# First modulation units of 512 shift and 512 scale columns, three projection blocks by quarters of K, x loaded first, unit 4 on TensorE

## The chip, the core and the metric

The kernel runs on one core of a Trainium2 chip. Its engines are TensorE (matrix products), VectorE, ScalarE, GpSimd and SyncE (SP), which here only starts DMAs; the core's 16 DMA engines move the data. The metric is the device time of one execution in microseconds, as the median of several runs.

## The reference

Two blocks of a network on 256 tokens of 2048 features, in float32. The change is in the first stages of the first block:

```python
mod = silu(c) @ w_ada + b_ada            # 12288 columns: six parts of 2048
shift_mix, scale_mix, gate_mix, shift_ffn, scale_ffn, gate_ffn = split(mod, 6)
h = modulate(rmsnorm(x, g_norm_mix), shift_mix, scale_mix)   # h * (1 + scale) + shift
u = h @ w_in                             # 2048 x 3072: lru, pool and gate columns, 1024 each
lru: causal conv of width 4, two gates by heads of 64, recurrence, times gelu(gate columns)
pool: four sliding means minus the input, times w_pool
x = x + gate_mix * (concat(lru, pool) @ w_out)
x = x + gate_ffn * ffn(modulate(rmsnorm(x), shift_ffn, scale_ffn))
```

The second block (state space and attention mixer, its own feed-forward, and a gated embedding) follows and is not touched.

## The kernel before

**Modulation.** The 12288 columns of `w_ada` are taken in twelve units of 1024 columns (`MOD_COLS`); a unit is 16 tiles of 128 rows of K, 512 KB each. Units 0 and 1 are the shift of the first norm, 2 and 3 its scale. `MOD_ORDER` (line 157) takes the first four as 0, 2, 1, 3, so that after two of them shift and scale of features 0 to 1023 are there, and after four the rest. For these TensorE multiplies: `mod_product` (line 1702) is two matmuls of 32 columns of weights by 512 (four instructions in the trace, since float32 takes two passes) for each tile, and two neighbouring tiles use different columns of the array. ScalarE then copies the sums to `mod_rows` (`mod_out`, line 1021 on), TensorE turns them to features by partitions (`mod_turn`, line 1690), VectorE adds the bias (`first_result`). The tiles come by SP's queue into eight slots (`load_first`, line 623), each asked for when the product eight before is done. `x` is loaded behind tile 4 and tile 5.

The other eight units are paced: `mod_places` says how many of their tiles stand at each place of `w_in` and `w_out`. GpSimd starts their loads into six slots (line 600), the first when all 64 first products are done. Units 5 and 6 are multiplied by TensorE in pairs of tiles (`mod_pair`, line 1719), the others, unit 4 among them, by VectorE into `mod_acc` (line 2464), and summed over partitions by TensorE (`mod_sums`, line 1663).

**Norm and `w_in`.** `x` is squared and scaled by ScalarE into `xn`, turned by TensorE (`turn_block`) into `features`. Two chunks of features at a time (`q`), VectorE applies gain and shift (`scaled`), ScalarE rounds to the high part `a_hi` (`norm_high`), VectorE takes the rest `a_lo` (`norm_low`). `w_in` is 6 blocks of 512 columns; each block is 8 halves, a half being 2 chunks of K. A 1 MB tile of `w_in` holds two halves and comes by SP's queue into one of four slots of `raw` (`load_tile`). Each half is split by ScalarE (`split_hi`, L845) and VectorE (`split_lo`, L2242) into high and low parts, three halves ahead of TensorE, and multiplied with 24 matmuls (`features_half`, lines 1538 to 1540: high by high, low by high, high by low). So each multiplies 8 times a line for a half, and the whole of `w_in` is 48 halves.

Halves are counted by places. Places 0 to 15 are blocks 0 and 1 done together: halves 0 to 3 of block 0, then of block 1 (the first half of K, which the first two units allow), then halves 4 to 7 of both. Six of the first four stand beside the first products at `W_IN_AT`, two after them. From place 8 on, `mods_beside` puts the pairs of paced tiles between the halves, one place behind (`MOD_LAG`). Block 0 and 1 are the lru columns: their conv taps are read from PSUM by VectorE (L2405) and must be done before block 2 or 3 writes the same bank of `pair`. The gates' products (line 1814) stand behind block 2, those of the pool (line 1790) in block 5. Then `w_out`, four blocks of eight halves (lines 1556 to 1558), its last instructions being `mod_joint` (line 1676).

All engines run in the order written here and wait for each other by semaphores.

Of the kernel before, what the change touches and what calls it, by code (L numbers as in the profile page):

```python
# [26 lines left out]
P = 128  # L27
# [60 lines left out]
def two_blocks(nc, d, out):  # L88
# [55 lines left out]
    def ya_slot(k):  # L144
# [69 lines left out]
    with ExitStack() as ctx:  # L214
# [38 lines left out]
        xn_sq = at("xn_sq", F + 32, [P, T, D])  # L253
# [14 lines left out]
        mod_more = [at("mod_more_0", 88, [P, 2, MOD_COLS]), at("mod_more_1", 104, [P, 2, MOD_COLS])]  # L268
# [237 lines left out]
        MOD_TURN_AT = [(1, 8), (2, 3), (3, 3)]  # L506
        TURN0_AT, W_IN_AT = [(1, 9), (1, 13), (2, 1), (2, 4)], [(2, 12), (2, 15), (3, 2), (3, 5), (3, 8), (3, 11)]
# [42 lines left out]
        def _(pool):  # L550
# [71 lines left out]
        def _(sp):  # L622
            def load_first(s):
                if s >= FIRST_SLOTS:
                    sp.wait_ge(mod_used, s - FIRST_SLOTS + 1)
                sp.dma_start(first_slot(s), ada[:, s % KC, bass.ds(MOD_ORDER[s // KC] * MOD_COLS, MOD_COLS)]).then_inc(mod_landed[s % FIRST_SLOTS], 16)
# [38 lines left out]
            sp.dma_start(c_rows[0:KC, :], by_chunk(d["c"][0])).then_inc(c_landed, 16)  # L665
            def load_in(b, j):
# [4 lines left out]
            w_in_at = {2 * KC + 3: 0, 2 * KC + 9: 1, 2 * KC + 15: 2, 3 * KC + 5: 3}  # L671
            for s in range(MOD_FIRST * KC):
# [159 lines left out]
        def _(act):  # L832
# [69 lines left out]
            def norm_sums(n, b):  # L902
# [3 lines left out]
                else:  # L906
                    mod_out(MOD_SUMS.index(7) + 1, JOINT_USED, misc[:, 3, :])
# [120 lines left out]
            def first_out(i):  # L1028
                mod_out(i, KC * (i + 1), first_bank(i))
# [5 lines left out]

            act.wait_ge(vec_turned, 1)
# [2191 lines left out]
```

## Time and profile before

| | us |
|---|---|
| median of 3 runs | 2527.49 (2527.4 to 2527.76) |
| span of the profiled execution | 2526.6 |
| TensorE busy in it | 2496.0 |
| VectorE busy | 1631.2 |
| ScalarE busy | 1257.4 |

The profile gives for each engine its busy time and, for each idle time, which engine or transfer ended it. The granted clock is TensorE's, as a share of 2.4 GHz. The DMA share is the mean busy share of the 16 DMA engines; queue q1 is the one that SP's loads use, q0 the one of GpSimd's. A matmul's row has its start and its modelled length; as matmuls overlap, the distance from start to start is what one costs.

### The profile page before, as it was taken

The numbers are of one execution on the slowest core, as the hardware profiler recorded it, in microseconds if no ns is written. First come the engines' busy times: TensorE is split into PE (matmuls) and PEld (weight loads), VectorE is DVE, ScalarE is ACT, GpSimd is POOL, SyncE is SP. The second block draws the span as 40 slices with busy tenths as digits, with TensorE's granted clock in tenths as the row PEclk, the third lists the DMA queues.
The fourth block names the chain that finished last, engine by engine and source line by source line (L and its number), as shares of the span: only waits on it lengthen the run. The fifth ranks groups of instructions, "written<-read, shape, count | busy, mean of one in ns | idle before, by whom it ended". The sixth has DMA issues, their size and how long they took to land.

```text
span 2526.6 us, 31728 instructions
## 1 busy us (share of the span) xinstructions
PE 2496.0 (99%) x12066; PEld 2032.2 (80%) x12066; DVE 1631.2 (65%) x1989; ACT 1257.4 (50%) x1665; POOL 78.7 (3%) x165
## 2 busy tenths in 40 slices
PE   7999999999999999999999999999999999999999
PEld 1688878888888888888888888888888888888887
DVE  1468998765555555565788678556777777755545
ACT  2354455444444444454566656445555555544463
POOL 0012210100000000000000000000000000000000
PEclk9999999999999999999999999999999999999999
DMA  9999998976666666675544554766777777766664
GB/s 383 394 345 384 358 353 295 327 262 221 213 219 220 201 215 211 211 217 176 167 132 132 179 192 167 229 206 229 237 247 238 240 237 241 237 210 203 212 233 133
DMA packets 401644, 600.34 MB, mean 238 GB/s; under 512 B 20944, under 2 KB 244208, under 8 KB 401024
## 3 DMA queue, kind: packets, MB, share of 16 engines
q1 hardware_dynamic: 381024, 525.66, 62.9%
q0 software_dynamic: 19616, 71.34, 7.5%
q10 hardware_dynamic: 896, 1.84, 0.3%
q8 instruction: 74, 1.21, 0.2%
q14 instruction: 34, 0.28, 0.0%
HBM read 573.84 MB, written 24.94 MB: 237 GB/s over the span
## 4 chain that ended last, share of the span: by engine, by line
PE 93%; DMA 3%; DVE 2%; ACT 1%; issue 1%; SPq 0%; POOL 0%; DVEq 0%; ACTq 0%
PE pair L1556 28%; PE pair L1558 27%; PE pair L1557 27%; DMA mod_raw<-in_w_ada 2%; PE pair L1538 1%; PE misc L1706 1%; PE pair L1539 1%; PE pair L1540 1%; DVE w_lo L2242 1%; PE misc L2102 1%; PE misc L1940 1%; DMA mod_page<-in_w_ada 0%; PE misc L1931 0%; PE misc L1919 0%; DMA mod_more<-in_w_ada 0%
## 5 line engine op out<-in xcount | busy, mean ns | idle before, releaser
L2242 DVE TENSOR_TENSOR w_lo<-raw,w_hi 128x1024 fp32r<-128x1024 f32 x848 | 1015.1, 1203 | 739.3 <-ACT w_hi L845 736.7
L845 ACT ACTIVATE w_hi<-raw 128x1024 fp32r<-128x1024 f32 x848 | 882.5, 1043 | 954.6 <-PE pair L1558 869.3
L1556 PE MATMUL pair<-w_hi,a_hi 128*128 128x512 f32 x2016 | 791.3, 393 | 0.8 <-DVE w_lo L2242 0.7
L1558 PE MATMUL pair<-w_hi,a_lo 128*128 128x512 f32 x2016 | 785.1, 389 | 0.0
L1557 PE MATMUL pair<-w_lo,a_hi 128*128 128x512 f32 x2016 | 784.5, 389 | 0.0
L1556 PEld LDWEIGHTS pair<-w_hi,a_hi 128*128 128x128 f32 x2016 | 378.4, 188 | 82.8 <-issue 2.9
L1558 PEld LDWEIGHTS pair<-w_hi,a_lo 128*128 128x128 f32 x2016 | 378.4, 188 | 79.2
L1557 PEld LDWEIGHTS pair<-w_lo,a_hi 128*128 128x128 f32 x2016 | 378.6, 188 | 77.4 <-issue 0.5
L1556 PE MATMUL pair<-w_hi,hid_hi 128*128 128x512 f32 x704 | 274.0, 389 | 0.0
L1558 PE MATMUL pair<-w_hi,hid_lo 128*128 128x512 f32 x704 | 273.9, 389 | 0.0
L1557 PE MATMUL pair<-w_lo,hid_hi 128*128 128x512 f32 x704 | 273.9, 389 | 0.0
L1557 PEld LDWEIGHTS pair<-w_lo,hid_hi 128*128 128x128 f32 x704 | 132.1, 188 | 27.6
L1556 PEld LDWEIGHTS pair<-w_hi,hid_hi 128*128 128x128 f32 x704 | 132.1, 188 | 27.6
L1558 PEld LDWEIGHTS pair<-w_hi,hid_lo 128*128 128x128 f32 x704 | 132.1, 188 | 27.3
L1538 PE MATMUL pair<-a_hi,w_hi 128*128 128x256 f32 x384 | 111.6, 291 | 1.4 <-DVE xc L2405 1.1
L1539 PE MATMUL pair<-a_lo,w_hi 128*128 128x256 f32 x384 | 108.5, 283 | 0.0
L1540 PE MATMUL pair<-a_hi,w_lo 128*128 128x256 f32 x384 | 108.5, 283 | 0.0
L1538 PEld LDWEIGHTS pair<-a_hi,w_hi 128*128 128x128 f32 x384 | 73.4, 191 | 18.2 <-issue 13.5
L2464 DVE SCALAR_TENSOR_TENSOR mod_acc<-mod_raw,keep,mod_acc 128x1024 f32<-128x1024 f32 x60 | 76.7, 1278 | 11.1 <-DMA mod_raw<-in_w_ada 10.3
L1539 PEld LDWEIGHTS pair<-a_lo,w_hi 128*128 128x128 f32 x384 | 73.6, 192 | 0.1
L1540 PEld LDWEIGHTS pair<-a_hi,w_lo 128*128 128x128 f32 x384 | 73.5, 191 | 0.0
L600 POOL DMA_DIRECT2D mod_raw<-in_w_ada x86 | 45.6, 531 | 337.4 <-DVE mod_acc L2464 146.3
(400 smaller groups left out, 2165.6 us busy)
## 6 DMA issues: line engine op xcount, KB each, us to landing
raw<-in_w_in SPq DMA_DIRECT2D x88, 1024.0 KB, 5.4
raw<-in_w_up SPq DMA_DIRECT2D x176, 512.0 KB, 4.4
raw<-in_w_out SPq DMA_DIRECT2D x48, 1024.0 KB, 5.7
raw<-in_w_ffn_gate SPq DMA_DIRECT2D x88, 512.0 KB, 3.6
raw<-in_w_ffn_up SPq DMA_DIRECT2D x88, 512.0 KB, 4.6
mod_raw<-in_w_ada POOLq DMA_DIRECT2D x86, 512.0 KB, 7.5
raw<-in_w_ffn_down SPq DMA_DIRECT2D x32, 1024.0 KB, 5.1
raw<-in_w_down SPq DMA_DIRECT2D x32, 1024.0 KB, 5.1
```

The costliest lines, as they stand in the source:

```text
L600: pool.dma_start(mod_slot(n), ada[:, k, bass.ds(a * MOD_COLS, MOD_COLS)]).then_inc(page_landed[mod_landing(n)[0]], 16)
L845: run(w_hi[:, h % HALF_SLOTS, 0:n, :], raw[:, h // 2 % RAW_SLOTS, at0:at0 + n, :], ACT.Copy).then_inc(hi_ready, 1)
L1538: pe.matmul(o, wh, hi[:, k, :], start=(kh == kk == 0 and m % 2 == 0), stop=False, skip_group_check=True)
L1539: pe.matmul(o, wh, lo[:, k, :], start=False, stop=False, skip_group_check=True)
L1540: mm = pe.matmul(o, wl, hi[:, k, :], start=False, stop=(kh == ph.halves - 1 and kk == n - 1), skip_group_check=True)
L1556: pe.matmul(o, hi[:, own], w_hi[:, slot, kk, :], start=(h == kk == 0), stop=False)
L1557: pe.matmul(o, hi[:, own], w_lo[:, slot, kk, :], start=False, stop=False)
L1558: mm = pe.matmul(o, lo[:, own], w_hi[:, slot, kk, :], start=False, stop=(h == ph.halves - 1 and kk == n - 1))
L1706: mm = pe.matmul(bank[own], c_silu[:, k:k + 1].to_broadcast([P, P // 4]), tile[:, e * COLS:(e + 1) * COLS], start=(k < 2), stop=(k >= KC - ...
L1940: mm = pe.matmul(misc[HD * e:HD * (e + 1), 2 + q, 3 * P:], v_t[:, k, n, :], p_tr[:, i % 2, e, keys], start=(k == 0), stop=(k == q), skip_g ...
L2242: dve.tensor_tensor(w_lo[:, slot, 0:n, :], raw[:, h // 2 % RAW_SLOTS, at0:at0 + n, :], w_hi[:, slot, 0:n, :].bitcast(F32), ALU.subtract).t ...
L2464: dve.scalar_tensor_tensor(out=acc, in0=of, scalar=by, in1=acc, op0=ALU.mult, op1=ALU.add).then_inc(mod_step, 1)
```

## The change

- **Units.** Each of the first four units `u` now holds 512 shift columns and the 512 scale columns of the same features (`by_quarter`). A tile is still 512 KB, in two pieces of 512 columns for each row of K. After unit `u` the features of quarter `u` can be finished: `first_result`, gain and `scaled` work by quarters.
- **`w_in`.** Blocks 0, 1 and 2 are done together by quarters of K: six halves for each quarter (`in_half`). Halves 6(u-1) to 6(u-1)+4 stand beside the products of unit `u` (`W_IN_AT`), the sixth behind its `mod_turn`; the last six follow unit 3. Block 2 is accumulated in `misc[:, 0:2]`, blocks 0 and 1 in `pair`. SP puts three tiles of `w_in` in each unit's loads.
- **`x` first.** `x` is loaded ahead of the first tile, and `xn` is computed by VectorE. The vectors are turned after product 6 and the features at products 7, 9, 11 and 13 of unit 0.
- **Paced units.** Unit 4 goes to TensorE. `mods_by_place` states the tiles of each place (D for VectorE, P for TensorE), from place 18 on. GpSimd's first six loads wait for 57 to 62 products instead of 64. The eight first slots lie elsewhere (`mod_more` in one piece).
- **Around it.** Conv, gates (behind place 26), pool and gelu steps keep their order and stand at new places.

```diff
-    mod_places = [0] * 8 + [0, 3, 1, 3, 0, 2, 0, 3] + [1, 2, 1, 2, 1, 0, 1, 1] + [1, 3, 2, 1, 1, 1, 2, 1] + [3, 2, 2, 2, 0, 2, 1, 2] \
-        + [2, 1, 3, 2, 1, 1, 2, 1] + [2, 1, 1, 2] + [1, 1, 1, 2] * 6 + [0] * 4 + [1, 0] * (4 * up1.halves)
-    MOD_ORDER = [0, 2, 1, 3]
-    MOD_BY_PE, MOD_BY_DVE = [5, 6], [4, 7, 8, 9, 10, 11]
+    FIRST_BLOCKS = 3
+    FIRST_HALVES = 2 * FIRST_BLOCKS
+    FIRST_PLACES = FIRST_BLOCKS * w_in.halves
+    PACED = FIRST_PLACES - FIRST_HALVES - 1
+
+    mods_by_place = [""] * (PACED + 1) + ["DPP", "DPP"] + ["PP"] * 6 + ["D", "DD", "D", "PP", "DPP", "D"] \
+        + ["PP", "D", "PP", "PP", "PP", "PP", "PP", "D"] + ["PP", "D", "PP", "D", "D", "PP", "PP", "D"] \
+        + ["DPP", "D", "DPP", "DD", "DPP", "D", "DPP", "DD"] + ["D", "D", "D", "DD"] * 4 + ["D"] * 4 + [""] * 4
+    mod_places = [len(m) for m in mods_by_place]
+    MOD_BY_PE, MOD_BY_DVE = [5, 4, 6], [7, 8, 9, 10, 11]
...
     def in_half(p):
 
-        b, h = divmod(p, w_in.halves)
-        return (b, h) if b >= 2 else (h // 4, 4 * b + h % 4)
+        q, n = divmod(p, FIRST_HALVES)
+        return divmod(p, w_in.halves) if p >= FIRST_PLACES else (n // 2, 2 * q + n % 2)
...
+        def in_bank(block):
+
+            return misc[:, 0:2] if block == FIRST_BLOCKS - 1 else pair[:, 1 - block % 2] if block < FIRST_BLOCKS else pair[:, block % 2]
...
-        MOD_TURN_AT = [(1, 8), (2, 3), (3, 3)]
-        TURN0_AT, W_IN_AT = [(1, 9), (1, 13), (2, 1), (2, 4)], [(2, 12), (2, 15), (3, 2), (3, 5), (3, 8), (3, 11)]
+        TURN0_AT, W_IN_AT = [7, 9, 11, 13], {3: (0, 1), 7: (2,), 11: (3,), 15: (4,)}
+        GATES_AT = 26
...
                 if n < MOD_SLOTS_LATER:
-                    pool.wait_ge(mod_used, FIRST_TILES)
+
+                    pool.wait_ge(mod_used, FIRST_TILES - FIRST_SLOTS + n + 1)
...
-                sp.dma_start(first_slot(s), ada[:, s % KC, bass.ds(MOD_ORDER[s // KC] * MOD_COLS, MOD_COLS)]).then_inc(mod_landed[s % FIRST_SLOTS], 16)
+                u, k = divmod(s, KC)
+                sp.dma_start(first_slot(s).rearrange("p (e n) -> p e n", e=2),
+                             by_quarter(ada[:, k, 0:2 * D], u)).then_inc(mod_landed[s % FIRST_SLOTS], 16)
...
-            w_in_at = {2 * KC + 3: 0, 2 * KC + 9: 1, 2 * KC + 15: 2, 3 * KC + 5: 3}
+            w_in_at = {u * KC + s: FIRST_BLOCKS * u + n for u in range(MOD_FIRST) for n, s in enumerate((12, 15, 19))}
...
             pe.wait_ge(c_ready, 1)
-            for i in range(MOD_FIRST):
+            for u in range(MOD_FIRST):
+                p = FIRST_HALVES * (u - 1)
                 for k in range(KC):
-                    first_product(i, k)
...
+                    first_product(u, k)
+                    if u == 0:
+                        if k == 6:
+                            turn_vectors()
+                        elif k in TURN0_AT:
+                            turn_block(0, TURN0_AT.index(k))
+                    else:
+                        for n in W_IN_AT.get(k, ()):
+                            if (u, n) == (1, 4):
+
+                                pe.wait_ge(n_f, XB)
+                            half_in(p + n)
+                mod_turn(u, u + 1)
+                if u:
+                    half_in(p + FIRST_HALVES - 1)
...
+            for u in range(MOD_FIRST):
+                p = FIRST_HALVES * u
+                split_in(range(max(0, p - 2), p + 2))
+                first_result(u)
+                dve.wait_ge(mod_ready, u + 1)
+                modulated_gain(mod[:, KC:2 * KC], g_mix, slice(4 * u, 4 * u + 4))
+                for q in (2 * u, 2 * u + 1):
+                    scaled(q)
+                for q in (2 * u, 2 * u + 1):
+                    norm_low(q)
+                if u < MOD_FIRST - 1:
+                    split_in(range(p + 2, p + 4))
+                if u == 0:
+                    prepare_lru()
+                    prepare_cosines()
```

## Rows read from the trace of the kernel before

**Rows 1.** The page: busy time of engines, and the span in 40 slices

```profile
PE   7999999999999999999999999999999999999999
...
DMA  9999998976666666675544554766777777766664
```

**Rows 2.** TensorE's waits, before 76 us, then 149.8 to 364: us, times, longest

```profile
PE pair L1706 <- DMA mod_more<-in_w_ada: 7.4, 11, 2.7
PE pair L1706 <- DMA mod_raw<-in_w_ada: 4.6, 7, 2.2
...
PE pair L1556 <- DVE w_lo L2242: 0.9, 2, 0.5
```

**Rows 3.** Stretches: length; busy PE, PEld, DVE, ACT, POOL; clock, DMA share, GB/s

```profile
2.00:8.00 6.00, 3.13 (x11) 0.77 (x13) 0.00 (x0) 0.28 (x2) 2.40 (x17) 1.00 0.94 342
...
60.00:80.00 20.00, 15.36 (x78) 6.28 (x80) 7.50 (x14) 5.15 (x7) 0.00 (x0) 0.83 1.03 402
...
96.00:104.00 8.00, 8.00 (x60) 5.72 (x57) 1.23 (x1) 0.02 (x1) 0.00 (x0) 1.00 1.03 404
104.00:108.00 4.00, 3.26 (x29) 1.62 (x28) 0.00 (x0) 0.60 (x1) 1.05 (x2) 1.00 1.05 388
...
300.00:320.00 20.00, 20.00 (x96) 16.66 (x95) 19.89 (x19) 9.99 (x13) 4.23 (x8) 1.00 1.04 399
...
149.80:363.90 214.10, 212.66 (x1358) 182.77 (x1356) 180.40 (x173) 106.10 (x135) 40.66 (x77) 1.00 0.97 363
0.00:149.80 149.80, 127.06 (x787) 70.50 (x788) 52.75 (x106) 49.88 (x61) 15.65 (x46) 0.94 1.01 382
```

**Rows 4.** TensorE from 149.8 to 364 us, groups by line: count, busy us, mean ns

```profile
L1538 PE MATMUL pair<-a_hi,w_hi 128*128 128x256 f32 x240 | 69.6, 290 | 0.0
L1706 PE MATMUL misc<-mod_raw,keep 128*32 128x512 f32 x68 | 10.6, 603 | 0.0
L1706 PE MATMUL misc<-mod_page,keep 128*32 128x512 f32 x28 | 5.3, 603 | 0.5 <-DMA mod_page<-in_w_ada 0.5
L1667 PE MATMUL misc<-ones,mod_acc 128*128 128x1 f32 x32 | 3.8, 248 | 0.0
```

**Rows 5.** TensorE in order of time: start us, us, what, count, idle before

```profile
107.32 1.05 PE L1698 MATMUL misc<-keep,mod_rows 128*128 128x2 f32 x8 [0.74 <-ACT mod_rows L1026]
...
123.35 1.06 PE L1706 MATMUL misc<-mod_raw,keep 128*32 128x512 f32 x8
124.35 0.39 PE L1538 MATMUL pair<-a_hi,w_hi 128*128 128x256 f32 x1
...
149.82 0.28 PE L1538 MATMUL pair<-a_hi,w_hi 128*128 128x256 f32 x1
...
363.94 1.06 PE L1676 MATMUL misc<-mod_acc,ones 128*32 128x512 f32 x8
```

**Rows 6.** DMA queues in 110 to 111, then 111 to 112 us: packets, MB, share

```profile
q1 hardware_dynamic: 200, 0.39, 105.8%
...
q0 software_dynamic: 61, 0.25, 63.4%
q1 hardware_dynamic: 66, 0.13, 35.0%
```

**Rows 7.** GpSimd in order of time

```profile
106.95 2.24 POOL L600 DMA_DIRECT2D mod_raw<-in_w_ada  x4 [75.30 <-PE misc L1706]
```

**Rows 8.** VectorE and ScalarE in order of time behind the last turn

```profile
108.82 1.45 DVE L2500 TENSOR_SCALAR features<-features,keep,mod 128x256 f32<-128x256 f32 x4
110.33 0.69 DVE L2338 TENSOR_TENSOR a_lo<-features,a_hi 128x512 fp32r<-128x512 f32 x1
...
109.66 1.28 ACT L932 ACTIVATE a_hi<-features 128x512 fp32r<-128x512 f32 x2 [2.39 <-DVE features L2500]
```

**Rows 9.** DMA of 120 to 160 us: mean, and GpSimd's issues with landing in us

```profile
DMA packets 7342, 14.25 MB, mean 356 GB/s; under 512 B 2425, under 2 KB 2425, under 8 KB 7338
...
mod_raw<-in_w_ada POOLq DMA_DIRECT2D x12, 512.0 KB, 9.9
```

More of the change, by code:

```diff
@@ L665, in _ @@
             sp.dma_start(c_rows[0:KC, :], by_chunk(d["c"][0])).then_inc(c_landed, 16)
+            for t in range(T):
+                sp.dma_start(x[:, t, :], d["x"][0, t * P:(t + 1) * P, :]).then_inc(x_landed, 16)
             def load_in(b, j):
@@ L689, in load_gates @@
                              w.rearrange("(m e) i j -> e i m j", e=2)[e]).then_inc(mixw_landed, 16)
-            for b in range(1, w_in.blocks):
-                if b == 2:
+            for b in range(FIRST_BLOCKS, w_in.blocks):
+                if b == FIRST_BLOCKS:
                     sp.wait_ge(zeroed, 2)
@@ L1046, in _, with split_in, prepared @@
[L1046 to L1048 removed]
+            def split_in(places):
+                for p in places:
+                    ph, b, h = in_or_out(p)
+                    split_hi(ph, b, [h])
+            def prepared():
+                act.wait_ge(prep_in, 1)
+                run(l_exp, l_abs, ACT.Exp, scale=-1.0).then_inc(prep_exp, 1)
+                act.wait_ge(prep_in, 2)
+                run(half_sin, ang_r, ACT.Sin, scale=0.5).then_inc(prep_exp, 1)
+                run(sin_t, ang_r, ACT.Sin).then_inc(prep_exp, 1)
@@ L1065, in mixer @@
-            def mixer(b):
-                for n in range(w_in.halves):
-                    h = LEAD + n
-                    ph, b1 = (w_in, b) if h < w_in.halves else (w_in, b + 1) if b + 1 < w_in.blocks else (w_out, 0)
-                    split_hi(ph, b1, [h % w_in.halves])
-                    if (b, n) == (1, 4):
-                        act.wait_ge(w_used, w_in.half(1) + 4)
-                        conv_bias(0, 0, cw1[:, (CONV - 1) * RC:], cb1, xc, c1_bias)
-                    beside(b, n)
-                    rows_beside(b * w_in.halves + n)
-                act.wait_ge(w_used, w_in.end(b))
@@ new lines, in beside @@
+            def beside(p):
+                if p == 20:
+                    act.wait_ge(w_used, 20)
+                    conv_bias(1, 0, cw1[:, (CONV - 1) * RC:], cb1, xc, c1_bias)
+                elif p == 22:
+                    act.wait_ge(w_used, 22)
+                    conv_bias(0, 4, cw1[:, (CONV - 1) * RC:], cb1, xc, c1_bias)
+                elif p == 24:
+                    act.wait_ge(w_used, 24)
+                    run(flat(xp[:, 0:4, :]), flat(misc[:, 0:2, :]), ACT.Copy).then_inc(xp_ev, 1)
+                elif p == 26:
+                    run(std, var, ACT.Sigmoid)
+                elif p == 27:
+                    for m in range(RC):
+                        act.wait_ge(gate_mm, m + 1)
+                        run(lru_a[:, m, :], misc[:, m % 3, 0:S], ACT.Sigmoid, bias=b_ra[:, m:m + 1]).then_inc(gate_ev, 1)
+                        run(lru_u[:, m, :], misc[:, m % 3, S:2 * S], ACT.Sigmoid, bias=b_ri[:, m:m + 1]).then_inc(gate_ev, 1)
+                elif p == 29:
@@ L2624, in pooled_out @@
                                              op0=ALU.mult, op1=ALU.subtract).then_inc(pool_lo_ev, 1)
-            for b in range(1, w_in.blocks):
-                mixer(b)
+            for p in range(PACED, IN_PLACES):
+                split_in([p + LEAD])
+                beside(p)
+                mod_beside(p)
             pooled_out(range(6, 2 * G))
```

248 lines of the change are left out of this document (99 added, 149 removed).

## The prediction

> **What bounds the kernel now.** I read the page first, then TensorE's waits by stretch, then the stretches with their granted clock and DMA rate, then TensorE's own order of time. The page says that TensorE is busy for 99% of the span and that only the first of the 40 slices is open, and that the DMA engines are full in the first seven slices, up to about 440 us [rows 1]. The reader is to see that the change touches only the first 364 us: the last 32 tiles of the paced units and all that comes after `w_out` keep their count and order. TensorE waits for `w_ada` tiles by DMA 12.0 us before 76 us in the two largest groups alone (7.4 + 4.6), and between 149.8 and 364 us it waits 1.4 us in all (0.9 for VectorE, 0.5 for a tile) [rows 2, 4]. So up to the first half of `w_in` at about 76 us DMA sets the pace and TensorE has room, and after it TensorE does: 214.1 us with 212.7 busy [rows 3, 4].
>
> The time is therefore a sum of two parts: when TensorE gets to a fixed place of its work, and how much it still has to do from there. I take as that place the start of half 18 of the 48 halves of `w_in` (the place from which the new code goes on by blocks, and the last quarter of K begins). Before, it starts at 149.82 us; 240 of the 384 matmuls of line 1538 are left (30 halves of 8), and 96 of line 1706, 4 instructions to a tile, so 24 tiles or 12 pairs [rows 4, 5]. From there to the end of `w_out`, the matmuls of line 1676 at 363.94, it is 214.1 us.
>
> **The change, part by part.**
>
> Bytes before the last first-unit tile. The 64 tiles of 512 KB are 33.55 MB, `x` 2.10 MB. SP now puts ten 1 MB tiles of `w_in` (10.49 MB) ahead of tile 63, against four before. Sum 46.1 MB. They all run on queue q1.
>
> Rate. A tile of `w_ada` is now two pieces of 512 columns in each row, so its runs in HBM are 2 KB and no longer 4 KB; those of `w_in` are 2 KB already. At 96 to 104 us, with nearly only 4 KB runs moving, the row gives 404 GB/s; at 104 to 108, with only `w_in` tiles in flight, 388, at a full share in both [rows 3]. I take 388 for the 44.0 MB and 404 for `x`, whose runs are longer: 113.4 + 5.2 us. The start costs 3.7 us, an estimate: 2 us and some before the first transfer, and of the 2 to 8 us at 342 GB/s [rows 3] one us is lost. So without any rival traffic tile 63 lands at 3.7 + 5.2 + 113.4 = 122.3 us. The ends are 404 GB/s for all (117.8 us) and 388 with the same start loss as now (123.7).
>
> The Trainium skill (DMA: Bandwidth & Descriptors, "Why small descriptors are slow") tells of a fixed cost of some 3 cycles a packet beside one cycle for each 32 bytes. By that 2 KB would cost 67 cycles twice where 4 KB costs 131, or 2.3%, and 44 MB would take 110.2 us at the rate of the 4 KB row less 2.3%, 3 us less than by the row. The trace shows 4%, and the sum goes by the trace.
>
> GpSimd's tiles. POOL now asks for the first six tiles of the paced units when 57, 58 ... products are done, not after 64. Before, its first request was issued at 106.95 us and its queue q0 moved nothing until 111; in the microsecond 110 to 111 q1 had 200 packets, in the next q0 had 61 and q1 66 [rows 6, 7]. So the data follow some 4.5 us behind the request, and then the two queues take turns packet by packet, with 4 KB on q0 against 2 KB on q1: q0 gets 0.25 MB of each us and q1 0.13. In the new order product 56 comes after half 14, at about 115.5 us (tile 55 lands at 3.7 + 5.2 + 38.8 MB / 388 GB/s = 108.9, but TensorE is at halves 12 and 13 until 110, does products 52 to 55 in 2 us, half 14 until 115). Pool data then flow from 120. Of q1 0.8 MB are still to come, and at 0.13 MB/us that takes 6 us in place of 2: tile 63 lands at 126. The ends: 122 if the requests come late enough to miss it, 130 if all six tiles (3.1 MB, 8 us at 390) go ahead of it.
>
> TensorE in the same stretch. A half is 24 matmuls at 0.12 us, 2.88 us; a pair of products 0.99 us start to start (123.35 to 124.35) [rows 4, 5]. A unit has 16 products (8 us in pairs, some more when they come one by one), a turn of 1.0 and six halves of 17.3: 27 us. DMA needs for a unit 8.39 + 3.15 MB at 388, 29.7 us. So 18 halves (52 us of work) lie beside transfers where 6 did; TensorE has some 2.5 us of room in each unit. ScalarE and VectorE have 6 splits of 1.04 and 1.2 us in a unit of 30 us each, and the normalisation of `x` that moves from ScalarE to VectorE is early and hidden by the arrival of unit 0. The turn of the vectors moves from after product 13 to after product 6 and may wait for small loads until some 22 us; eight tiles are in flight by then, so no transfer is late.
>
> From tile 63 to half 18: product 0.98, half 16 2.88 (it covers ScalarE's copy of the rows), turn 1.05, half 17 2.88; in all 7.8. Beside half 17 runs the chain bias, gain, four scalings 1.45, high part 0.63, low part 0.69, which before took from the turn's end at 108.37 to 111.0 [rows 5, 8]: 2.7 us, hidden with 0.2 to spare. What comes next if it is late is the same wait, tenths of a us. Half 18 then starts at 126 + 7.8 = 133.8, against 149.8: 16.0 us earlier.
>
> Unit 4 on TensorE. Sixteen tiles are eight more pairs, and unit 6's all lie behind half 18 too, as do all of unit 5's: 24 pairs after it against 12 before. 12 x 0.99 = 11.9 us, and all of it on the path, since TensorE is full there. For unit 4 the sums over `mod_acc` (line 1667: 3.8 us for two units) give way to a turn of 1.0: 0.8 less or so [rows 4, 5]. VectorE is freed of 16 x 1.28 us, worth nothing unless it is the bound; in `w_out`, where it is busy 19.9 of 20 us [rows 3], it has 34 tiles against 36, and TensorE waits for it 0.9 us [rows 2]. The four gates' loads (small runs), the conv taps, gates and pool steps move by some places; each stands again three or more halves ahead of its reader. I cost them at nothing; 0.5 us each if not.
>
> Waits behind half 18. The eight pairs of places 18 to 25 are read every 3.87 us from six slots, so a slot has 11.6 us from read to next read; landing takes a median of 9.9 us in the stretch 120 to 160 [rows 9], and issue another 0.5 to 1. Most are in time by a us; the first pair after the six that are in hand is asked for at 141 and read at 147, 1 to 2 us late. I put 3 us for all such waits, where before has 1.4. Bounds 0 and 8.
>
> **Sum.** -16.0 + 11.9 - 0.8 + 1.6 = -3.3 us on the profiled span of 2526.6, 2523.3; the median of the three runs, 2527.5, lies 0.9 above that span, so 2524.2.
>
> **The rivals.**
>
> B, DMA is quicker than I take it: 2 KB runs at 404 GB/s (-4.4 us), q0 doesn't overtake (-4), or one of these with fewer waits behind half 18. Against it speak [rows 3, 6]; for it, that in `w_out`, with both kinds of runs mixed, 399 is reached. One and a half of these: -3.3 - 6.5, 2517.7.
>
> C, slower: DMA becomes the bound of the whole stretch to the end of `w_out`. Before, 57.2 MB were in by 149.8 us and 77.7 came after (382 and 363 GB/s [rows 3]). Of the same 134.9 MB now 50.7 are in at 133.8, and 84.2 are left for 226.6 us, a mean of 372 GB/s, where 363 at a share of 0.97 was moved before and 399 in the best part. The work decides for TensorE down to 366 GB/s at the cost of the gain; at 356, the mean of 120 to 160 us with the gates' loads [rows 9], 84.2 MB take 236.5 us, end 370.3, so +6.4: 2533.9. For it: q1 and q0 are both full in `w_out` already. Against: the last 4.2 MB are tiles of `up1` that need not be in by then, and the ten slots hold 7.3 MB in hand.
> The Trainium skill (same page, "Where 436 GB/s comes from") says that the HBM side binds at some 358 GB/s for each core. By that C would hold, with 84.2 MB in 235 us and 2532.4. The rows of 404 and 399 GB/s here speak against it, so it adds nothing to C's chance.
>
> D, slower: the halves aren't hidden by the transfers. If TensorE has a clock of 0.83 (between its two levels of 1.2 and 2.4 GHz), as in the stretch 60 to 80 us [rows 3], the 82 us of work in the three units take 17 us more, of which 7.5 are room: +9.5, 2533.7. Before 76 us single waits are as long as 2.7 and 2.2 us; from 96 us on, where they are short, the clock is 1.00 [rows 2, 3]. The new order fills such gaps, so this is unlikely. Also here: that the change doesn't do what it says, and a quarter's first halves wait for the chain of mod rows, so that fewer than 18 are done when tile 63 lands; each half that is left costs 2.9.
>
> **How the numbers follow.** Forecast 0.46 (2520 to 2528), B 0.27, C 0.16, D 0.11. A measurement of this kernel tells some 0.2%, 5 us, from no change. Faster by more than that: a third of the forecast's chance and nearly all of B, 0.41. Slower: two thirds of C, most of D, 0.20. Same: 0.39. The range leaves a tenth on either side: 2514 to 2534.
>
> **What would show it.** In the profile after: the first matmul of line 1538's kind at 39 to 43 us; DMA at 385 to 395 GB/s from 12 to 110 us; tile 63's products at 124 to 130; half 18 at 132 to 138; 24 pairs in place of 12 behind it with about 11 us more of line 1706's work; the end of `w_out` at 358 to 363; 2163 us from there as before. Wrong if the DMA rate of the first 110 us is over 400 or under 375, if q0 moves nothing before tile 63, if TensorE waits more than 8 us behind half 18, or if anything after `w_out` changes length.

## The result, and the profile after

| | before | after |
|---|---|---|
| median, same chip | 2527.73 us (2527.36 to 2529.11) | 2535.35 us (2533.46 to 2537.32) |
| profiled execution: time, span | time not kept, 2526.6 | 2535.05, 2533.3 |
| half 18 of `w_in` starts | 149.82 | 141.41 |
| `w_out` ends | 363.94 | 370.59 |

The ratio is 1.0029, with a 95% interval of 1.002 to 1.0038: slower, by 7.6 us. The prediction was 3.3 us faster; its range ended at 2534. The traces of the two kernels differ by less, 6.7 us. Wherever both are kept, the time is 1.7 to 2.0 us above the span, so the execution behind the trace of before took some 2528.3 us (an estimate), 0.6 above its median here. Lines moved: the products are L1724, the matmuls of a half L1556 to L1558, the turn L1716, GpSimd's loads L616.

First the place the prediction named, half 18. TensorE of the changed kernel in order of time, from the first half of `w_in` to the last quarter of K (start, length, what, count, idle before and what ended it):

```profile
39.44 5.79 PE L1724 MATMUL misc<-mod_raw,keep 128*32 128x512 f32 x16 [0.95 <-DMA mod_raw<-in_w_ada]
45.16 0.39 PE L1556 MATMUL pair<-a_hi,w_hi 128*128 128x256 f32 x1
...
123.41 1.05 PE L1724 MATMUL misc<-mod_more,keep 128*32 128x512 f32 x4 [1.27 <-DMA mod_more<-in_w_ada]
127.13 1.92 PE L1724 MATMUL misc<-mod_more,keep 128*32 128x512 f32 x4 [2.66 <-DMA mod_more<-in_w_ada]
130.96 1.92 PE L1724 MATMUL misc<-mod_more,keep 128*32 128x512 f32 x4 [1.91 <-DMA mod_more<-in_w_ada]
132.81 0.58 PE L1556 MATMUL misc<-a_hi,w_hi 128*128 128x256 f32 x1
...
136.18 0.41 PE L1556 MATMUL misc<-a_hi,w_hi 128*128 128x256 f32 x1
136.39 0.41 PE L1557 MATMUL misc<-a_lo,w_hi 128*128 128x256 f32 x1
...
141.41 0.28 PE L1556 MATMUL pair<-a_hi,w_hi 128*128 128x256 f32 x1
...
147.26 1.06 PE L1724 MATMUL misc<-mod_raw,keep 128*32 128x512 f32 x8
151.32 1.06 PE L1724 MATMUL misc<-mod_page,keep 128*32 128x512 f32 x8
```

The first half of `w_in` starts at 45.16 us, where the prediction had 39 to 43: the first four products of unit 1 take 5.8 us, mostly at the low clock. That was made up for, since TensorE waits for tiles again at 63 us. The last two rows are pairs of paced tiles, with one half behind each. The last three tiles of the 64 come 2.3 to 3.8 us apart. Behind the wait of 2.66 us a product takes 1.92 us in place of 1.05, and in half 16 two matmuls stand 0.21 us apart in place of 0.12: half 16, from 132.81 to the turn at 137.64, lasts 4.8 us and not 2.9. The stretches show the clock (columns as in [rows 3]):

```profile
20.00:40.00 20.00, 13.61 (x84) 6.08 (x82) 6.62 (x18) 7.16 (x9) 1.81 (x1) 0.95 1.05 385
40.00:60.00 20.00, 20.00 (x136) 12.27 (x133) 10.01 (x29) 8.07 (x11) 0.00 (x0) 0.88 1.05 387
...
126.00:130.00 4.00, 1.92 (x4) 0.18 (x4) 0.00 (x0) 0.00 (x0) 0.00 (x0) 0.60 1.03 399
130.00:134.00 4.00, 3.04 (x9) 1.38 (x10) 0.00 (x0) 0.60 (x1) 0.00 (x0) 0.50 1.03 399
134.00:138.00 4.00, 4.00 (x25) 4.00 (x24) 0.00 (x0) 0.00 (x0) 0.00 (x0) 0.62 1.05 386
...
141.30:370.60 229.30, 225.78 (x1449) 184.15 (x1447) 175.46 (x179) 111.30 (x145) 47.68 (x90) 1.00 0.96 358
```

From 130 to 134 us the granted clock is 0.50, the lower of its two levels, 1.2 GHz. In the first rows, with 2 KB runs, DMA gives 385 to 387 GB/s where before has 402 to 404 [rows 3]. GpSimd's requests, and what the queues did in 122 to 124 us:

```profile
117.30 2.25 POOL L616 DMA_DIRECT2D mod_raw<-in_w_ada  x4 [93.46 <-PE misc L1724]
122.45 0.53 POOL L616 DMA_DIRECT2D mod_page<-in_w_ada  x1 [2.91 <-PE misc L1724]
...
q0 software_dynamic: 143, 0.52, 66.3%
q1 hardware_dynamic: 139, 0.28, 36.3%
```

143 packets of the one and 139 of the other queue: they take turns, and GpSimd's are nearly twice as large (3.6 and 2.0 KB on average). While its tiles come, the first 64 get 36% of the engines' time.

Behind half 18, the waits of TensorE in 141 to 371 us:

```profile
PE misc L1724 <- DMA mod_raw<-in_w_ada: 2.8, 2, 1.9
PE misc L1724 <- DMA mod_page<-in_w_ada: 0.8, 1, 0.8
```

So half 18 came 8.4 us earlier than before, not 16.0, and the way from there to the end of `w_out` is 229.2 us where it was 214.1; TensorE is busy for 225.7 of them. From there to the end both kernels take 2162.7 us.

### The profile page after: what moved, and what is told of

Same layout as the page of the kernel before. It is cut to its first block, busy times and chain, and to the rows that moved or that the text cites. A ratio compares the mean times of both kernels' runs of the same rounds, so it can differ in the third digit from the quotient of the medians.

```text
span 2533.3 us, 31826 instructions
## 1 busy us (share of the span) xinstructions
PE 2496.7 (99%) x12122; PEld 2033.6 (80%) x12122; DVE 1619.1 (64%) x1977; ACT 1254.8 (50%) x1664; POOL 78.8 (3%) x165
## 4 chain that ended last, share of the span: by engine, by line
PE 94%; DMA 3%; DVE 1%; SPq 1%; ACT 0%; issue 0%; POOL 0%; DVEq 0%
PE pair L1574 27%; PE pair L1576 27%; PE pair L1575 27%; PE misc L1724 2%; DMA mod_more<-in_w_ada 2%; PE pair L1556 1%; DMA mod_raw<-in_w_ada 1%; PE pair L1557 1%; PE pair L1558 1%; PE misc L2117 1%; PE misc L1955 1%; PE misc L1946 0%; PE misc L1934 0%; PE misc L1556 0%; PE misc L1557 0%
## 5 line engine op out<-in xcount | busy, mean ns | idle before, releaser
L1556 PE MATMUL pair<-a_hi,w_hi 128*128 128x256 f32 x320 | 93.4, 292 | 0.0
L1557 PE MATMUL pair<-a_lo,w_hi 128*128 128x256 f32 x320 | 90.4, 283 | 0.0
L1558 PE MATMUL pair<-a_hi,w_lo 128*128 128x256 f32 x320 | 90.4, 282 | 0.0
L1556 PEld LDWEIGHTS pair<-a_hi,w_hi 128*128 128x128 f32 x320 | 61.1, 191 | 18.3 <-issue 16.6
L2479 DVE SCALAR_TENSOR_TENSOR mod_acc<-mod_raw,keep,mod_acc 128x1024 f32<-128x1024 f32 x53 | 67.8, 1279 | 10.5 <-DMA mod_raw<-in_w_ada 10.2
L1557 PEld LDWEIGHTS pair<-a_lo,w_hi 128*128 128x128 f32 x320 | 61.3, 192 | 0.1
L1558 PEld LDWEIGHTS pair<-a_hi,w_lo 128*128 128x128 f32 x320 | 61.2, 191 | 0.0
L616 POOL DMA_DIRECT2D mod_raw<-in_w_ada x86 | 45.7, 533 | 348.0 <-PE misc L1724 156.7
```

The lines of the kernel that those rows point to most:

```text
L616: pool.dma_start(mod_slot(n), ada[:, k, bass.ds(a * MOD_COLS, MOD_COLS)]).then_inc(page_landed[mod_landing(n)[0]], 16)
L1556: pe.matmul(o, wh, hi[:, k, :], start=(kh == kk == 0 and m % 2 == 0), stop=False, skip_group_check=True)
L1557: pe.matmul(o, wh, lo[:, k, :], start=False, stop=False, skip_group_check=True)
L1558: mm = pe.matmul(o, wl, hi[:, k, :], start=False, stop=(kh == ph.halves - 1 and kk == n - 1), skip_group_check=True)
L2479: dve.scalar_tensor_tensor(out=acc, in0=of, scalar=by, in1=acc, op0=ALU.mult, op1=ALU.add).then_inc(mod_step, 1)
```

## The experiments

A run is compared with runs of the kernel before on the same chip (medians 2527.59 to 2528.20). Where experiments are compared with each other, it is by their distance to it, "+7.6" for the changed kernel.

**GpSimd's early requests.** In the changed kernel, then in the kernel before.

```diff
# e1_pool_after_64: the changed kernel
-                    pool.wait_ge(mod_used, FIRST_TILES - FIRST_SLOTS + n + 1)
+                    pool.wait_ge(mod_used, FIRST_TILES)
# e5_before_early_pool: the kernel before
-                    pool.wait_ge(mod_used, FIRST_TILES)
+                    pool.wait_ge(mod_used, FIRST_TILES - FIRST_SLOTS + n + 1)
```

> Edit: the changed kernel, but GpSimd asks for its first six tiles only when all 64 first products are done. Theory Q (queue q0 takes two thirds of the bytes from q1 while both have work, so tile 63 is 6 us late, and the longer waits take TensorE's clock down for product 63 and half 16, 3 us more; behind half 18 TensorE is the bound): tile 63's product starts at 124 to 126 instead of 131, half 16 takes 2.9 us, half 18 starts at 132 to 134, time 2526 to 2529, 7 to 9 us below the changed kernel. Rival T (the transfers are the bound all the way to the end of w_out, so the same bytes only come in another order): half 18 is earlier, but the waits behind it grow by as much, time 2533 to 2537.

2530.53 us, ratio 1.001 (1.0 to 1.0019): +2.3, so 5.3 us better than the changed kernel. Half 18 came as theory Q said, the time (2526 to 2529) did not; it lies between the two theories. TensorE in order of time, then two stretches, then its waits from 132.7 to 366.4 us:

```profile
125.09 1.05 PE L1724 MATMUL misc<-mod_more,keep 128*32 128x512 f32 x4 [0.30 <-DMA mod_more<-in_w_ada]
126.07 0.38 PE L1556 MATMUL misc<-a_hi,w_hi 128*128 128x256 f32 x1
...
132.81 0.28 PE L1556 MATMUL pair<-a_hi,w_hi 128*128 128x256 f32 x1
...
276.00:280.00 4.00, 2.40 (x9) 0.73 (x10) 0.74 (x1) 0.19 (x1) 0.03 (x1) 0.70 0.99 372
280.00:284.00 4.00, 4.00 (x22) 3.35 (x20) 3.23 (x4) 0.69 (x1) 2.07 (x4) 0.87 1.04 409
...
PE misc L1724 <- DMA mod_raw<-in_w_ada: 3.9, 3, 2.6
PE misc L1829 <- DMA gates_w<-in_w_rg_i: 1.3, 1, 1.3
PE misc L1724 <- DMA mod_page<-in_w_ada: 1.0, 1, 1.0
```

Tile 63's product starts at 125.09 and not 130.96, the clock stays at 1.00 there, and half 18 starts 8.6 us earlier. The end of `w_out` comes only 4.3 us earlier (366.34): the stretch behind half 18 grew from 229.2 to 233.5. 2.6 us of that are more waits (6.2 in place of 3.6), 1.7 the lower clock behind the wait of 2.6 us for one tile, in the two stretches above (4 x 0.30 + 4 x 0.13).

What else differs at half 18 is how much GpSimd's queue has brought by then. Queue q0 from 0 to the start of half 18, in the changed kernel and in e1:

```profile
q0 software_dynamic: 864, 3.15, 5.7%
q0 software_dynamic: 137, 0.54, 1.2%
```

In the changed kernel all six of its first tiles are in, in e1 one.

> Edit: the kernel before, but GpSimd asks for its first six tiles when 57 to 62 products are done. Theory Q: data of q0 flow from about 100.5 us; q1 has 1.4 MB to go to tile 63 and with packets of 4 KB on both queues gets half, so tile 63 is 3 to 4 us later, and since everything behind it is TensorE's work the end is 3 us later: 2530 to 2532. Rival T: the bytes that q0 brings early are missing from later waits (in all 2.5 us between 107 and 280 us before), no change, 2527 to 2529.

2528.62 us, ratio 1.0002 (0.9992 to 1.0012): +1.0. The expected loss of 3 us isn't there; the expectation of no change held. Half 18 starts at 150.6 (149.82), `w_out` ends at 364.23. TensorE of this kernel at the last products, and the queues in 102 to 108 us:

```profile
100.35 1.91 PE L1706 MATMUL misc<-mod_raw,keep 128*32 128x512 f32 x12
...
105.25 1.92 PE L1706 MATMUL misc<-mod_more,keep 128*32 128x512 f32 x16
...
q1 hardware_dynamic: 554, 1.31, 56.8%
q0 software_dynamic: 297, 1.09, 46.1%
```

GpSimd's tiles take nearly half of the engines' time here too. But TensorE does three and four products in a row behind a half and waits for none: the tiles lay ready, and had room to be late. Half 18 is 0.8 us late, of which 0.6 stood before GpSimd's first request (the product at 88.83 us in the kernel before is at 89.43). In the changed kernel TensorE stands at the last three tiles one by one, so each us of delay is a us of its own. The same edit costs 1.0 us, inside the noise, in one order and 5.3 in the other.

**Runs of 2 KB.** In the kernel before the 64 first tiles read as two pieces of 512 columns; in the changed kernel with the edit of e1 as whole rows of 1024.

```diff
# e4_before_2kb: the kernel before
-                sp.dma_start(first_slot(s), ada[:, s % KC, bass.ds(MOD_ORDER[s // KC] * MOD_COLS, MOD_COLS)]).then_inc(mod_landed[s % FIRST_SLOTS], 16)
+                u, k = divmod(s, KC)
+                sp.dma_start(first_slot(s).rearrange("p (e n) -> p e n", e=2),
+                             ada[:, k, 0:2 * D].rearrange("p (e n) -> p e n", e=2)[:, :, COLS * u:COLS * (u + 1)]).then_inc(mod_landed[s % FIRST_SLOTS], 16)
# e11_64_4kb_runs: e1_pool_after_64
-                sp.dma_start(first_slot(s).rearrange("p (e n) -> p e n", e=2),
-                             by_quarter(ada[:, k, 0:2 * D], u)).then_inc(mod_landed[s % FIRST_SLOTS], 16)
+                sp.dma_start(first_slot(s), ada[:, k, bass.ds(u * MOD_COLS, MOD_COLS)]).then_inc(mod_landed[s % FIRST_SLOTS], 16)
```

> Edit: the kernel before, but the first 64 tiles are read as two pieces of 512 columns a row (so in runs of 2 KB); this leaves wrong modulation values, the amount of work is the same. Theory R (2 KB runs move at 388 GB/s, 4 KB ones at 404 to 409): 33.55 MB take 3.4 to 4.5 us more, the tile that ends the first stage is that much later and so is the end: 2531 to 2532.5. Rival: the rate of the first stage is hidden, time 2527.7 as before.

2532.23 us, ratio 1.0016 (1.0006 to 1.0026): +4.0, as theory R said. The first stretch of the profile:

```profile
20.00:40.00 20.00, 17.34 (x62) 2.38 (x58) 2.93 (x18) 11.12 (x13) 1.80 (x1) 0.86 1.05 386
```

Half 0 is at 80.1 us in place of 75.8, half 18 at 153.6, the end of `w_out` at 367.7: the 4 us are lost before the first half and carried to the end unchanged.

> The changed kernel with GpSimd's first six requests behind product 64 (as e1_pool_after_64) and the first 64 tiles of w_ada read as whole rows of 1024 columns, so in runs of 4 KB in place of 2 KB; the modulation is therefore that of other columns. Same bytes and tiles. Theory R (the 2 KB runs cost some 4 us, in the changed kernel as in the kernel before, and as they are time of the DMA engines they reach the end of w_out): DMA 400 to 410 GB/s in 20 to 100 us, half 18 at 128 to 130 us where e1_pool_after_64 had 132.8, end of w_out 362 to 363.5 (366.3), median 2526 to 2527.5. Rival S (TensorE bounds the first 130 us as soon as DMA is quicker, since 18 halves now stand there): half 18 at 131.5 or later, median 2529 to 2530.5. Rival W (what is won by half 18 is given back as waits for the paced tiles): half 18 at 128 to 130, more than 7 us of waits for tiles behind it, median 2529 to 2530.5.

2526.48 us, ratio 1.0 (0.999 to 1.0009): -1.7, 4.0 better than e1. A stretch of it, and its waits behind half 18:

```profile
40.00:60.00 20.00, 20.00 (x144) 13.30 (x144) 9.29 (x28) 7.61 (x11) 0.00 (x0) 0.95 1.04 404
...
PE misc L1723 <- DMA mod_raw<-in_w_ada: 4.1, 4, 1.6
PE misc L1828 <- DMA gates_w<-in_w_rg_i: 1.6, 1, 1.6
PE misc L1723 <- DMA mod_page<-in_w_ada: 1.1, 2, 0.7
```

Theory R held in each number except the end of `w_out`, which beat it (361.12 against 362 to 363.5). Half 18 starts at 128.4. So the runs of 2 KB cost 4.0 us in either kernel. And here nothing of what half 18 won (4.4 us) was given back: `w_out` ends 5.2 us earlier than in e1. With both parts taken out the changed kernel is level with the kernel before: 5.3 + 4.0 us stand against its loss of 7.6, and the 1.7 that the rest of the change brings can't be told from nothing (0.999 to 1.0009).

**Unit 4 on VectorE.** Two placings of its sixteen tiles; a third follows further down. In e2 they keep their places, in e6 they are spread; e3 and e7 are these with the edit of e1. The steps that sum unit 4 and add it up (`ROWS_AT`, `SUMS_AT`, `RESULT_AT`) follow its new places; their lines are left out below.

```diff
# e2_unit4_dve
-    mods_by_place = [""] * (PACED + 1) + ["DPP", "DPP"] + ["PP"] * 6 + ["D", "DD", "D", "PP", "DPP", "D"] \
-        + ["PP", "D", "PP", "PP", "PP", "PP", "PP", "D"] + ["PP", "D", "PP", "D", "D", "PP", "PP", "D"] \
+    mods_by_place = [""] * (PACED + 1) + ["DPP", "DPP"] + ["PP"] * 6 + ["D", "DD", "D", "DD", "DDD", "D"] \
+        + ["DD", "D", "DD", "DD", "DD", "DD", "DD", "D"] + ["PP", "D", "PP", "D", "D", "PP", "PP", "D"] \
...
-    MOD_BY_PE, MOD_BY_DVE = [5, 4, 6], [7, 8, 9, 10, 11]
+    MOD_BY_PE, MOD_BY_DVE = [5, 6], [4, 7, 8, 9, 10, 11]
# e6_unit4_dve_spread: the same two lines of places become
+    mods_by_place = [""] * (PACED + 1) + ["DPP", "DPP", "PP", "DPP", "PP", "DPP", "PP", "PP"] + ["DD", "DDD", "DD", "D", "DD", "DD"] \
+        + ["PP", "DD", "PP", "", "PP", "", "PP", "D"] + ["D", "DD", "DD", "DD", "DD", "D", "D", ""] \
# e3_both, e7_spread_and_64: e2 and e6, each with
-                    pool.wait_ge(mod_used, FIRST_TILES - FIRST_SLOTS + n + 1)
+                    pool.wait_ge(mod_used, FIRST_TILES)
```

> Edit: the changed kernel, but unit 4 is back on VectorE, at the same places and with the same number of tiles at each. Theory P (TensorE is full behind half 18, so eight pairs of 0.99 us less and sums of 1.8 for a turn of 1.0 are worth 7 us): time 2527 to 2529, half 18 as in the changed kernel at 141.4. Rival T (transfers are the bound) or V (VectorE can't take 16 x 1.28 us more among its splits): waits for tiles or for w_lo take the place, time 2533 or more.

2539.73 us, ratio 1.0047 (1.003 to 1.0064): +11.5, 3.9 worse than the changed kernel: rival V held. TensorE's waits behind half 18, VectorE in order of time, and a stretch:

```profile
PE pair L1556 <- DVE w_lo L2257: 10.9, 5, 4.9
...
217.53 4.42 DVE L2582 TENSOR_TENSOR_SCAN xc<-lru_a,lru_u 128x2048 f32<-128x2048 f32 x1
221.86 1.26 DVE L2479 SCALAR_TENSOR_TENSOR mod_acc<-mod_raw,keep,mod_acc 128x1024 f32<-128x1024 f32 x1
223.22 1.28 DVE L2479 SCALAR_TENSOR_TENSOR mod_acc<-mod_page,keep,mod_acc 128x1024 f32<-128x1024 f32 x1
224.43 1.22 DVE L2257 TENSOR_TENSOR w_lo<-raw,w_hi 128x1024 fp32r<-128x1024 f32 x1
...
190.00:250.00 60.00, 49.15 (x386) 46.49 (x385) 58.77 (x57) 30.14 (x37) 11.64 (x22) 0.94 0.89 312
```

VectorE is busy for 58.8 of 60 us, and the low part of a half stands behind the scan of 4.42 us and two tiles: TensorE waits 4.9 us for it, and its clock falls (0.94 over the stretch). Less these 10.9 us of waits, the run is some 7 us shorter than the changed kernel. So unit 4 on TensorE takes load from an engine that had no room at these places; the prediction called that relief worth nothing unless VectorE is the bound.

> Edit: both of the last two at once. Theories Q and P together: the two gains add up, 14 to 16 us below the changed kernel, time 2519 to 2522, which would also be 6 to 8 us below the kernel before. Rival T: with TensorE's part 15 us shorter the transfers become the bound, and no more than half of the sum is left, time 2526 or more.

2535.79 us, ratio 1.0031 (1.0018 to 1.0044): +7.6, far from the 14 to 16 us of gain expected. Half 18 is at 132.8, and 9.9 us of waits for VectorE remain. The trace is of an execution of 2540.62 us, 4.8 above the median, so its waits are read with care; by the medians the later requests bring 3.9 here.

> Edit: the changed kernel with unit 4 on VectorE again, its tiles and those of unit 7 now at places where VectorE has room (none at 34 to 38, where the recurrence and the window sums stand; one beside some of the conv taps; eleven at 26 to 31), still 54 tiles in w_in and 42 in w_out. Theory P: without the 10.9 us of waits for w_lo that the plain move had, the 7 us of TensorE's work come off in full: half 18 at 141 as in the changed kernel, w_out's end 363 to 365, time 2527 to 2530. Rival T: waits for tiles take their place, 2533 or more.

2532.48 us, ratio 1.0019 (1.001 to 1.0029): +4.9, between the two theories. The waits for VectorE's low parts are gone; those for tiles are 7.7 us, the longest 3.7 at 277.4.

> Edit: the same, and GpSimd's first six tiles after 64 products. Theories P and Q: the gain over the run with the second edit alone is the same 7 us, 2522 to 2525, 4 to 6 us below the kernel before. Rival T (the transfers bound the stretch once TensorE's part is shorter; DMA has to bring the same 135 MB by then): 2527 or more, with waits for tiles of 4 us or more behind half 18.

2529.31 us, ratio 1.0008 (0.9999 to 1.0018): +1.7, as rival T said. Half 18 at 132.5, and now 11.5 us of waits for tiles. Its waits, and two stretches:

```profile
PE misc L1724 <- DMA mod_page<-in_w_ada: 5.8, 3, 3.0
PE misc L1724 <- DMA mod_raw<-in_w_ada: 5.7, 3, 4.0
...
240.00:260.00 20.00, 19.42 (x132) 18.19 (x132) 19.69 (x23) 8.72 (x14) 4.46 (x9) 1.00 0.97 353
260.00:280.00 20.00, 16.01 (x71) 10.58 (x71) 14.70 (x15) 7.89 (x9) 4.37 (x9) 0.91 0.84 311
```

DMA has a hole (0.84) directly beside the wait of 4.0 us at 275.1: as I read it, few tiles are read at the places ahead of it, so few slots come free and few loads are asked for, and then places with many tiles drain the slots. No run shows these steps one by one.

**The supply of tiles.** Halving what the paced tiles read (columns 0 to 511 of each tile from the seventh on), in e1 and in e7.

```diff
# e9_64_half_tiles: e1; e10_spread_half_tiles: e7
-                pool.dma_start(mod_slot(n), ada[:, k, bass.ds(a * MOD_COLS, MOD_COLS)]).then_inc(page_landed[mod_landing(n)[0]], 16)
+                cols = MOD_COLS if n < MOD_SLOTS_LATER or n >= TILES_UP1 else MOD_COLS // 2
+                pool.dma_start(mod_slot(n)[:, 0:cols], ada[:, k, bass.ds(a * MOD_COLS, cols)]).then_inc(page_landed[mod_landing(n)[0]], 16)
```

> Edit: the changed kernel with GpSimd's first six after 64 products, and of each paced tile from the seventh to the 96th only 512 of the 1024 columns are read (the modulation from them is wrong, every instruction on the engines stays): 23.6 MB less by the end of w_out. Theory S: the waits for tiles behind half 18 (3.7 us at 139 to 172, 2.6 at 277) go, 2523 to 2526. Rival P (TensorE's own work is the bound, the waits are slack that would be taken elsewhere): 2529 to 2531.

2523.45 us, ratio 0.9982 (0.9973 to 0.9992): -4.7, 7.1 better than e1, in theory S's range. The stretch from half 18 to the end of `w_out`, and its waits:

```profile
132.80:360.00 227.20, 225.55 (x1446) 184.03 (x1444) 175.64 (x179) 111.17 (x145) 48.37 (x90) 1.00 0.79 271
...
PE misc L1725 <- DMA mod_page<-in_w_ada: 1.6, 1, 1.6
```

With room in DMA (0.79), TensorE's busy time behind half 18, 225.6 us, is as in the changed kernel, and 6.3 us of e1's 7.9 us of waits and low clock go. That is rival C's mechanism, in part and not at its price (9.7 us above the forecast): behind half 18 the supply of tiles sets a part of the pace in e1.

> Edit: the same half reading in the kernel with unit 4 spread on VectorE and the first six after 64 products. Theory S: its 11.4 us of waits for tiles go, 2517 to 2520, and the difference to the run with half tiles and unit 4 on TensorE is then the full price of eight pairs, 6 to 8 us. Rival V (VectorE takes over as the bound, waits for w_lo): 2523 or more.

2520.89 us, ratio 0.9971 (0.996 to 0.9983): -7.3, 9.0 better than e7. It missed its 2517 to 2520: in the profiled execution, at 2523.61 its longest and 2.7 above the median, 5.4 us of waits for tiles remain, 3.2 of them at 269.2, for a tile of half the size. Bytes alone are then not the cause of that wait; when its slot came free, and what stood ahead of it on the queues, was not varied by itself, so that wait stays open.

**An even pace.** VectorE takes unit 4 and the places are laid so that the tiles read per us vary less; e8 with GpSimd's requests behind product 64, e12 with them early.

```diff
# e8_even_pace against the changed kernel; the lines of places taken out are left out here
# e12_even_early_pool: without the last pair of lines
+    mods_by_place = [""] * (PACED + 1) + ["DPP", "DPP"] + ["PP"] * 6 + ["DD", "DDD", "DD", "D", "DD", "DD"] \
+        + ["PP", "DD", "PP", "", "PP", "", "PP", "D"] + ["D", "DD", "DD", "DD", "DD", "DPP", "D", "DPP"] \
+        + ["DD", "D", "D", "DD", "DPP", "D", "DPP", "DD"] + ["D", "D", "D", "DD"] * 4 + ["D"] * 4 + [""] * 4
+    MOD_BY_PE, MOD_BY_DVE = [5, 6], [4, 7, 8, 9, 10, 11]
...
-                    pool.wait_ge(mod_used, FIRST_TILES - FIRST_SLOTS + n + 1)
+                    pool.wait_ge(mod_used, FIRST_TILES)
```

> Edit: unit 4 on VectorE and the first six after 64 products as in the last run, with another list of places: no tile of VectorE beside the conv taps, 57 tiles in w_in (two more pairs and one tile at 45 to 48, where the DMA engines had been idle for 15%) and 39 in w_out instead of 42. Theory S (the supply of tiles bounds the stretch wherever more than some 2 tiles stand at a place; the 11.4 us of waits for tiles of the last run come from triples at 21 and 23 and from the 18 tiles of w_out's first block): waits for tiles down to 4 us or less, 2520 to 2525. Rival T (the sum of bytes decides, not their places): waits only move, 2527 or more.

2523.33 us, ratio 0.9984 (0.9975 to 0.9994): -4.9, faster than both kernels, though its ten times spread from 2521.69 to 2528.9. The time is in theory S's range; its waits for tiles, 4.4 us, are a little over the 4 it gave. The stretches that had the hole, and its largest waits behind half 18:

```profile
240.00:260.00 20.00, 20.00 (x141) 16.90 (x140) 19.61 (x22) 6.98 (x10) 6.26 (x12) 1.00 1.01 373
260.00:280.00 20.00, 17.46 (x91) 13.28 (x90) 16.15 (x14) 10.52 (x12) 4.56 (x10) 1.00 1.04 400
...
PE misc L1724 <- DMA mod_raw<-in_w_ada: 2.2, 2, 1.5
PE misc L1724 <- DMA mod_page<-in_w_ada: 2.2, 3, 1.6
PE misc L1622 <- DMA w_first<-in_w_ple_proj: 1.7, 1, 1.7
```

DMA has no hole (1.01 and 1.04 where the changed kernel has 0.84 and 0.89), waits for tiles of `w_ada` are 4.4 us where e7 has 11.5, and the clock stays at 1.00. `w_out` ends at 357.98.

> e8_even_pace with GpSimd's first six requests again as in the changed kernel, behind products 57 to 62. Theory Q (these requests delay tile 63 by about 6 us and leave TensorE at its low level for product 63 and half 16, whatever the places behind): half 18 at 140 to 142 in place of 132.4; as in this list of places hardly a tile is waited for, most of the 8.5 us reach the end: median 2528 to 2531. Rival V (the stretch behind half 18 is bound by the supply of tiles, so that an earlier start of the paced tiles is given back in full): median 2523 to 2526.

2526.86 us, ratio 0.9994 (0.9984 to 1.0003): -1.3, 3.5 worse than e8, between the two theories and a hit of neither. Half 18 at 140.3 as Q said, 7.9 us later than in e8, but the end of `w_out` is only 3.4 later (361.40): behind half 18 stand 3.9 us of waits in place of 7.9. The only edit between the two is the paced tiles' early start. Against the changed kernel, which has the same early start, e12 is 8.9 us better, and TensorE is busy for 217.2 us behind half 18 in place of 225.7: that is what unit 4 costs on TensorE.

## Why the prediction was wrong

The step that failed is the start of half 18, put at 133.8 us: it came at 141.41, 7.6 us late, since tile 63 was late and the clock behind it low. The price of a pair adds most of the rest. The forecast put the end of `w_out` at 360.6 us; it came at 370.6. The 10.0 us by its own steps:

1. **Tile 63: 126 forecast, its product at 130.96. 5.0 us.** The rate was right (385 to 387 GB/s, forecast 388), and so was the mechanism: packets in turn, request to data 4 us. Two terms were mis-sized. Without GpSimd's traffic the forecast was 122.3; e1 shows 125.09, with 47.0 MB moved on q1 by 125 us and not 46.1. The 0.9 MB that were left out (small loads, and parts of the `w_in` tiles asked for behind tile 63) are 2.4 of the 2.8 us. And overtaking cost 5.9 us, not 4: when q0 began to flow at 121 us, q1 had 1.5 MB to bring to tile 63 and not 0.8.
2. **From tile 63 to half 18: 7.8 forecast, 10.45 measured. 2.65 us.** At full clock the sum was right (e1: 125.09 to 132.81, 7.7). The clock was left out. The sum had the turn and the halves at 1.00, and rival D had the low clock in the wrong place, in all three units. There it was low once, at 38 to 46 us, and TensorE had the room for it. In e1, with waits of 0.3 us at the same tiles, the clock stays at 1.00, so the late tiles brought it down; the waits in [rows 2] and the clock of 0.83 in [rows 3] stood together already before 76 us. A wait is to be priced with what the next matmuls cost behind it: here waits of 5.8 us brought 2.7 more.
3. **Twelve pairs at 0.99: 11.9 forecast.** The count was right, 48 instead of 24 tiles. But 0.99 us is from the pair's start to the half's start. In the changed kernel a pair and a half take 4.06 us from start to start (147.26 to 151.32) and a half alone 2.88, so a pair costs 1.18, and twelve 14.2, 2.3 us more. TensorE's busy time behind half 18 grew from 212.7 to 225.7: 13.0 us, where the sum had 11.9 - 0.8 = 11.1. That is 1.9 us of the miss.
4. **Waits behind half 18: 3 forecast, 3.6 measured.** Near in the changed kernel, but by luck: with half 18 at 132.8, close to the forecast's 133.8, e1 shows 6.2 us of waits and 1.7 of low clock. No run with this list of places and all tiles read whole has both the early half 18 and the short way behind it (forecast 226.8 us; 229.2, 233.5 in e1, 232.7 in e11). What delaying GpSimd's requests wins at half 18, the next stage gives back in part: 4.3 us of 8.6 in e1, 4.5 of 7.9 between e12 and e8. What quicker transfers win is kept (e11 against e1: 4.4 us at half 18, 5.2 at the end). So what is given back goes with the head start of the paced tiles (3.15 MB in by half 18 against 0.54 in e1 and 0.60 in e11), and not with an early half 18 as such.
5. **Unit 4 on TensorE.** Its cost is real, 8.5 us of TensorE's time (e12 against the changed kernel), but the plain alternative costs 10.9 us of waits for VectorE. The placing decides: with unit 4 on VectorE and the late requests, e8 is 6.6 us better than e7 (-4.9 against +1.7) by its list of places and the steps that follow it.
6. **Outside the span.** The forecast took 0.9 us from the span of the trace to the median; in the changed kernel's profiled execution it is 1.75. The 0.9 is the median of three runs less the span of an execution whose time was not kept, a mis-reading of 0.8 us.

One sum beside the forecast was off too: 44 MB at the rate of the 4 KB row less 2.3% take 111.5 us and not 110.2. The forecast doesn't use it.

The rivals: B is out, since 2 KB runs move at 385 to 387 GB/s in each stretch and q0 did overtake. C put the end of `w_out` at 370.3 us, and it came at 370.59, at 358 GB/s, near C's 356; that is luck. In the changed kernel tiles held TensorE up for 3.6 us only, and its own work filled 225.7 of 229.2 us. Where the paced tiles came late, C's mechanism cost 6.3 us of its 9.7 (e1, e9). D's price of 9.5 us was near, but not its place. None of them joined the three that came together: late tile, low clock, dearer pairs. Tile 63 at 130 us stood in the forecast as an end and a low clock in D, but not both.

Two rules of the Trainium skill bear on this. By DMA: Bandwidth & Descriptors, "Why small descriptors are slow", the runs of 2 KB would cost 2.3%, 2.5 us of 110, an estimate from its cycles. The runs show more, some 4 to 5%, and 4.0 us in both kernels: in 20 to 100 us 406 GB/s in the kernel before against 386 in e4, and 402 in e11 against 387 in e1. The measurement decides. By the same page of the Trainium skill, "Queues, rings and completion order", an engine goes from queue to queue a packet at a time. The trace agrees (143 and 139 packets in 2 us); what the page counts as a packet can't be told from these rows.

## What to carry to other kernels

When a stage is pulled forward, ask what sets the pace of the one behind it: here half of each us that was won by asking for the paced tiles later came back behind half 18 as waits, while what quicker transfers won was kept. With the load on the engine that has room, and even places, that way became shorter in all (e8). A second queue that starts before the last transfer on which all hangs takes turns with it by packets, so large packets elsewhere slow small ones here; the same early start costs next to nothing where the tiles lie ready ahead of their products (e5). And price an operation from start to start of its neighbours, with and without it, never from its own row.

## What the runs showed of the hardware

- Full DMA engines (share 1.03 to 1.05) move 406 GB/s from HBM in 20 to 100 us of the kernel before, where most runs are of 4 KB, and 386 with the 64 tiles at 2 KB too (e4); in the changed order 402 with the 64 first tiles in runs of 4 KB (e11) and 387 with 2 KB (e1).
- While both queues have work, q0 and q1 take turns by packets (143 and 139 in 2 us, in e5 144 and 140), and the bytes go by their sizes.
- Behind a wait of 2.66 us at 127 us the clock was 0.60, then 0.50; behind 2.6 at 277.6 in e1 0.70; behind 4.0 in e7 0.91 over 20 us. In e8 no wait behind half 18 is over 1.7 us, and the clock is 1.00 there. The length of one wait doesn't decide: in e12 a wait of 2.67 us has a product at full clock behind it (1.05 us), and only the next, behind 2.72 us more, takes 1.92. In the changed kernel waits of 2.24, 1.80 and 0.95 us between 29 and 39 us stand before a clock of 0.50 at 40 to 44. What decides stays open.
